# Filling TensorE's waits with unused matmuls: the norms and the pair normalizations of a two-layer diffusion block

## The reference

```
for l in range(2):
    h = rmsnorm(x) * g_mix * (1 + scale) + shift              # norm 0 of the layer
    p = h @ w_in                                              # three head groups
    a = neighbourhood_attention(rmsnorm(q), rmsnorm(k), v)    # 4 heads of 64, in pairs
    b = bidirectional_mlstm(...)
    c = latent_attention(...)                                 # 8 heads
    x = x + gate1 * (concat(a, b, c) @ w_out)
    h = rmsnorm(x) * g_ffn * (1 + scale) + shift              # norm 1 of the layer
    x = x + gate2 * (silu(h @ w_a) * (h @ w_b)) @ w_ffn_out
```

## Time and profile before

| | |
|---|---|
| Time, median of 3 runs | 2289.54 us (2289.2 to 2289.91) |
| The profiled execution's own time | 2291.66 us |
| Its span, first to last instruction | 2289.9 us |
| Mean granted TensorE clock | 0.955 |
| TensorE busy | 2082.4 us, 91% of the span, 11392 matmuls |
| VectorE busy | 1183.6 us, 52% |
| ScalarE busy | 751.4 us, 33% |
| GpSimd busy | 642.2 us, 28% |
| Chain of work that ended last | TensorE 78%, VectorE 10%, ScalarE 5%, issue 4% |

### The profile page before, as it was taken

One profiled execution on the slowest core, in us unless ns is written; L12 is line 12 of the kernel. 1 busy time (PEld: TensorE's weight loads), 2 busy tenths in 40 slices (PEclk: granted clock), 3 DMA queues, 4 the chain that ended last, 5 costly groups with the idle time before them and its releaser, 6 DMA issues.

```text
span 2289.9 us, 29294 instructions
## 1 busy us (share of the span) xinstructions
PE 2082.4 (91%) x11392; PEld 1714.8 (75%) x11392; DVE 1183.6 (52%) x2119; ACT 751.4 (33%) x1221; POOL 642.2 (28%) x820
## 2 busy tenths in 40 slices
PE   6787999988988899999999977889988888999999
PEld 4576888866666788888888866678866656878887
DVE  4457614457884767166526566563358865212212
ACT  4234223346653311111111233322355653212222
POOL 1200311221002233333333421131222004555555
PEclk8999989999999999999999989899899989999999
DMA  7300332110001233233323210011111001332322
GB/s 281 101 10 28 120 113 74 47 37 19 10 10 54 75 120 116 87 109 112 102 90 122 84 58 19 19 50 36 47 37 32 15 10 65 100 94 92 101 92 101
DMA packets 76239, 165.53 MB, mean 72 GB/s; under 512 B 5192, under 2 KB 46664, under 8 KB 75088
## 3 DMA queue, kind: packets, MB, share of 16 engines
q1 hardware_dynamic: 75728, 163.28, 21.5%
q10 hardware_dynamic: 384, 0.47, 0.1%
HBM read 161.63 MB, written 2.10 MB: 71 GB/s over the span
## 4 chain that ended last, share of the span: by engine, by line
PE 78%; DVE 10%; ACT 5%; issue 4%; POOL 1%; DMA 1%; PEld 0%; SPq 0%; PEldq 0%; DVEq 0%; ACTq 0%; POOLq 0%
PE psum L1054 22%; PE psum L1056 21%; PE psum L1055 21%; PE psum L1602 1%; DVE naptlo L1972 1%; POOL wlo L517 1%; PE psum L1136 1%; PE psum L1242 1%; DMA wm<-w_mod 1%; PE psum L1105 1%; PE psum L1371 1%; PE psum L1308 1%; PE psum L1357 1%; PE psum L1184 1%; PE psum L1309 1%
## 5 line engine op out<-in xcount | busy, mean ns | idle before, releaser
L517 POOL TENSOR_TENSOR wlo<-raw,whi 128x256 fp32r<-128x256 f32 x816 | 642.0, 819 | 1639.7 <-ACT whi L542 1639.7
L1054 PE MATMUL psum<-hhi,whi 128*128 128x512 f32 (+1 forms) x1640 | 589.6, 360 | 33.4 <-DVEq L1799 12.6
L1055 PE MATMUL psum<-hlo,whi 128*128 128x512 f32 (+1 forms) x1640 | 581.3, 354 | 0.0
L1056 PE MATMUL psum<-hhi,wlo 128*128 128x512 f32 (+1 forms) x1640 | 580.8, 354 | 0.0
L542 ACT ACTIVATE whi<-raw 128x1024 fp32r<-128x1024 f32 x204 | 215.5, 1059 | 929.8 <-PE psum L1056 929.4
L1054 PEld LDWEIGHTS psum<-hhi,whi 128*128 128x128 f32 x1640 | 314.8, 192 | 83.8 <-issue 26.7
L1056 PEld LDWEIGHTS psum<-hhi,wlo 128*128 128x128 f32 x1640 | 313.9, 191 | 43.1
L1055 PEld LDWEIGHTS psum<-hlo,whi 128*128 128x128 f32 x1640 | 314.9, 192 | 41.3 <-issue 0.5
L2401 DVE TENSOR_TENSOR ffuf<-ffsa,psum 128x768 f32<-128x768 f32 (+1 forms) x44 | 36.1, 821 | 337.3 <-ACT ffsa L1005 329.9
L2386 DVE SCALAR_TENSOR_TENSOR ffmacc<-wm,csil,ffmacc 128x256 f32<-128x256 f32 x336 | 189.6, 605 | 10.4 <-DVE ffmacc L2386 5.3
L1054 PE MATMUL psum<-uhi,whi 128*128 128x512 f32 (+1 forms) x528 | 189.0, 358 | 2.6 <-DVE ulo L2405 1.5
(11 more groups left out here) (324 smaller groups left out, 3362.5 us busy)
## 6 DMA issues: line engine op xcount, KB each, us to landing
raw<-w_stream SPq DMA_DIRECT2D x204, 512.0 KB, 3.6
wm<-w_mod SPq DMA_DIRECT2D x80, 512.0 KB, 3.9
wm<-w_mod SPq DMA_DIRECT2D x8, 1024.0 KB, 17.5
xres<-x_t SPq DMA_DIRECT2D x8, 384.0 KB, 6.0
out<-xres SPq DMA_DIRECT2D x8, 256.0 KB, 2.2
consts<-c_f SPq DMA_DIRECT2D x1, 353.0 KB, 7.7
narpb<-rpb ACTq DMA_DIRECT2D x2, 120.0 KB
mlmask<-c_gate ACTq DMA_DIRECT2D x2, 108.0 KB
```

What stands on the lines that cost most here:

```text
L517: nc.gpsimd.tensor_tensor(wlo[:, q % 2, c:c + UW // 4], raw[:, q % RAW, c:c + UW // 4], whi[:, q % 2, c:c + UW // 4], ALU.subtract).then_i ...
L1054: mm(dst, ah, bh, start=first, stop=False)
L1055: mm(dst, ah, bl, start=False, stop=False)
L1056: return mm(dst, al, bh, start=False, stop=last)
```

## The change

A helper `keep_warm(n)` issues n matmuls of the bf16 identity by itself, repeated to 256 columns, into the lower half of bank 0; nothing reads the result. It is called at these places of TensorE's stream: in both norms before an FFN 36 times ahead of the wait for the last squares, behind a new wait for the fifth updated tile; 42 times behind the statistics of every norm but the first; 40 times at the end of each pair's normalization, ahead of the barrier; and 24 times at the end of layer 0's FFN, behind a new wait for its last updated tile. These are 2 x 36 + 3 x 42 + 4 x 40 + 24 = 382 matmuls.

```diff
+            def keep_warm(n):
+
+                for _ in range(n):
+                    mm(bank(0)[:, 0:256], identb[:, :], identb[:, :].unsqueeze(1).broadcast_to([P, 2, P]), start=True, stop=True)
+
             def norm_phase(l, which, full):
                 if l == 0 and which == 0:
                     pe.wait_ge(const_in, 48)
                     pe.wait_ge(csil_zero, 1)
                     pe.wait_ge(act_chain, 1)
+                if which:
+                    pe.wait_ge(x_free, 2 + l * XPL + KT + 5)
+                    keep_warm(36)
                 pe.wait_ge(sq_used, 8 * (2 * l + which) + KT)
                 for r0, r1 in ranges(full):
                     ins = mm(psum_pair(psum, 3)[:, r0:r1], ones, norm_bufs(l, which)[1][:, 0, r0:r1], start=True, stop=True)
                 ins.then_inc(st_done, 1)
+                if l or which:
+                    keep_warm(42)
@@ na_pair
                 sums("kx", 1, NA["p"][:, 0, :], [(CTX_LEN, TOK)])
                 sums("kc", 1, NA["p"][:, 0, :], [(0, CTX_LEN)])
+                keep_warm(40)
@@ ff_pe, at its end
+                if full:
+                    pe.wait_ge(x_free, 2 + (l + 1) * XPL - 1)
+                    keep_warm(24)
```

## The result

| | before | changed |
|---|---|---|
| median of the runs shown (3 each) | 2289.54 (2289.2 to 2289.91) | 2275.94 (2272.74 to 2275.96) |
| profiled execution: time, span, clock | 2291.66, 2289.9, 0.955 | 2275.96, 2274.2, 0.974 |
| all runs: count, mean, lowest to highest | 46, 2290.7, 2281.2 to 2296.3 | 9, 2276.4, 2272.7 to 2279.5 |

The ratio is 0.9939, with a 95% interval of 0.9922 to 0.9957; in a second set of runs it was 0.9946 (0.9933 to 0.9959). So the kernel is faster: by 13.6 us between the medians shown, where the forecast said 7.95, and by 14.2 (give or take 1.6) between the means of all runs in the table. The measured median lies only 0.9 us inside the forecast's own range of 2275 to 2287. The last row tells why means are wanted: one and the same kernel spreads over 15 us. The three runs of before that stood ahead of the prediction lay 0.7 us apart by chance.

A forecast was written before the change was run, and what follows sets the result against it. It took the chain through TensorE, VectorE and ScalarE as the bound, with TensorE at half clock behind seven waits. Places -8.75, other stretches +0.8, total -7.95 from 2291.66: 2283.7; the median lying 2.1 lower, 2281.6, range 2275 to 2287.

The forecast's parts named there:

- Price of one filler: All filler blocks: one 256-column filler matmul takes 0.12 us, with 0.21 kept as the upper end.
- rival 2: All waits: the filler's weight load is not hidden, 0.21 us apiece; sum +23.3 us, 2312.8; chance 0.08.
- 3: All waits: the clock falls all the same, filler partly at 0.21, low stretches stay; +18.9 us, 2308; chance 0.04.
- Pairs of layer 0: Both layer 0 pairs: filler hidden behind VectorE's barrier, scores and transposes at full clock save 1.5 us each, -3.0 together.
- Pairs of layer 1: First pair: 0.8 us late against 0.9 won, -0.1; second pair: six transposes in about half the time, -0.8.
- Norm before layer 0's FFN: Filler hidden, statistics take 1.47 us instead of 2.93, VectorE's tiles and the matmuls end earlier; -2.3 us.
- First norm of layer 1: Statistics start 0.8 us late, then save 1.45; matmuls at 0.12 keep up with VectorE's tiles; -3.05 us.
- Norm before layer 1's FFN: Statistics already at full clock; filler delays them and the first matmul, then 48 matmuls at 0.23; +0.5 us.
- the last norm no better: Sign of being right: the norm before layer 1's FFN gains nothing, its term being +0.5 us.
- Sum of the seven places: Terms of the four pairs and three norms added: -8.75 us.
- The other low stretches: Low clock outside the seven places, 134 us: from two vanishing (-3.4) to four coming (+6.8); taken as +0.8 us.
- Rival 1: VectorE and ScalarE pace attention, so the pairs' 3.9 us go; two low stretches appear elsewhere (+3.4); 2288.1; chance 0.17.

The follow-up runs named there:

- the doubled kernel: Every filler block of the changed kernel doubled (72, 84, 80 and 48 matmuls); mean 2311.7 us, ratio 1.0093 to the kernel before.
- the two kernels with more filler: Changed kernel with layer 1's pairs cut to 34, last norm's 42 to 36, plus fillers in waits for POOL's weights; two sets: 2273.5 and 2269.0 us.

## Why the prediction was right in sign and range, and too small

- **Price of one filler, 0.12:** a little high: 0.109 from one start to the next, by (8.90 - 4.53) / 40. The estimate of 0.109 that the prediction worked out from the Trainium skill (TensorE: Matmul & The Clock Gate, "Back-to-back issue gap") is what the traces show. The weight load is hidden, so rival 2 is out; so are 3 (the clock is 1.00 under the filler) and 4.
- **Pairs of layer 0, -1.5 each:** 1.5 and 1.5 in every kernel that has them, hidden behind VectorE as said.
- **Pairs of layer 1, -0.1 and -0.8:** +0.2 and -0.5. The first pair's scores are 0.64 late where 0.8 was forecast (0.39 us of issue in the row of 1388.49) and win back 0.4, not 0.9, since the clock falls again 4.7 us behind their start; in the second pair it does 5.2 us behind.
- **Norm before layer 0's FFN, -2.3:** -2.1.
- **First norm of layer 1, -3.05:** -2.7 up to 1365 in all six profiles that have its filler, but 0.3 to 1.9 of it is given back by 1394. Up to 0.3 goes where a wait of 2.46 us in the bias products (first row below, its start the end of that wait) is followed by 6.8 us of low clock (second row, the table of windows of the changed kernel) instead of 3.4, in three of the six. In four of them another 1.5 to 1.6 goes to a second low stretch of 3.4 us some 14 us further on, which the kernel before does not have in any profile. What remains averages 1.6. I had looked for what is late next only as far as the end of the step.

```profile
1352.67 1.93 PE L1204 MATMUL psum<-narpb,consts 128*64 128x240 f32 x7 [2.46 <-DVE nabias L1932]
```

```profile
1352.26:1359.10 6.84, 6.21 (x26) 2.06 (x28) 5.62 (x14) 0.48 (x1) 5.21 (x8) 0.50 0.31 95
```

- **Norm before layer 1's FFN, +0.5:** wrong in sign: -1.0. The first filler is out when the statistics can start (0.1 late, not 0.5), the first matmul is 0.5 late and not 1.4, and the 48 matmuls run at 0.23 as said. That lateness makes 0.9 of the error of 1.5, and 0.5 is a wrong reading of the kernel before: the piece at 1928.51 of the chain is the 45th of the 48 matmuls, the one that POOL's next weights wait for, and I set it against the end of all 48. So one of the signs that I had named for being right, the last norm no better, did not come.
- **Sum of the seven places, -8.75:** -8.8 in the first pair of profiles, -8.0 in the mean. The errors of the terms cancel, so that the sum came out so close is luck.
- **The other low stretches, +0.8:** this is the term that was mis-sized, and wrong in sign: -6.9 in the pair of profiles, about -6 in the means. I bounded it by whole low stretches that vanish or come at 1.7 us each and put the near end at -3.4. The stretch from 222 to 373 alone gave 5.9 between the two profiles, 4.7 of it from the 10.2 us of low clock in the mLSTM's small products. About 3.8 of the 5.9 come with the change, which shifts the work; the rest is luck of the first profile of before. I had read low clock as something behind idle waits, and never looked at the stretches in which TensorE was busy.
- **Rival 1 (the gains do not last):** out. No row behind a place takes its gain back, and in the doubled kernel the losses of all seven places stay too.

What stays open: 8.0 in the places and 3.8 in 222 to 373 make 11.8 of the 14.2. The rest is near the error of the means; the row 373 to 737 points to it (a mean of 2.9 with layer 0's pairs filled, -0.9 without, apart from the two kernels with more filler), but its values jump by 4.4 within either group, so it isn't shown. Whether the clock sets in at random against the kernel's start, and why only some positions turn up (all six profiles with the filler stand within 0.5 us of each other), was not tried.

## What to carry to other kernels

A wait like the ones filled here (3.6 to 5.5 us) on TensorE's critical path is worth filling with real matmuls if they end before the wait does: the work just behind it then runs at 2.4 GHz. Half a block can gain as much where something else sets the pace behind it or where the whole block ends late, even though the clock falls. Price the filler by its lateness, since every 0.11 us past the wait stays in the total. And where a kernel's time depends on where low clock happens to fall, take several profiles and the mean of many runs before putting a few microseconds down to a cause: here one unaltered kernel ran from 2281.2 to 2298.5 us on two chips.

## What I had not expected of the hardware

- The clock is low while TensorE's records show no idle time: 30.6 us at 0.50 with 30.60 busy, with small products before and in it. There is no wait there to fill.
- A stretch without any filler gained up to 5.9 us by where its work stood when the clock fell; positions 0.6 to 3 us apart went with gains of 0, 1.9 to 4.1 or about 5.8 us.
- A block half as long gained as much time as a whole one in five places of seven, although in three of those five the clock fell in the wait or right behind it.
